# Four early first-layer tiles between the id transposes and the block's end, twelve spread over the gate steps

## The chip, the cores and the metric

The kernel runs on one core of a Trainium2 chip. The time is the device time of one execution in microseconds; lower is better. The engines are TensorE (PE, its weight loads PEld), VectorE (DVE), ScalarE (ACT), GpSimd (POOL) and SyncE (SP); the last three issue transfers.

## What is computed

One decoder layer on 256 prompt rows and 64 sample rows: projections, two kinds of attention, an output projection with LayerNorm, and then PEER, a retrieval over 128 x 128 single-neuron experts. The change lies in PEER:

```python
q = (xc @ wq).reshape(PEER_CHUNK, PEER_HEADS, PEER_DK)
s1, s2 = q[..., :half] @ k1, q[..., half:] @ k2        # scores, top 16 of each, top 16 of their sums
experts = jnp.take_along_axis(cidx, sel, axis=-1)       # 8 heads x 16 expert ids a row
g = jax.nn.softmax(sc, axis=-1)
hid = jax.nn.gelu(jnp.einsum('ced,cd->ce', u_tab[experts], xc))
y = jnp.einsum('ce,ced->cd', g * hid, v_tab[experts])
```

## The kernel before, in words

For the prompt rows the kernel does not gather experts. It multiplies x with all of u (the first layer, 128 tiles of 128 experts, each a weight tile of 128 x 1024 values), applies gelu, multiplies with a gate matrix W that is zero where a row did not choose an expert, and multiplies with all of v. The program is a series of blocks. In each block every engine has its own instruction stream, held together by semaphores, and a block's end is at the source line of the class that follows, L1096 in the profile.

`route_block` finds ids and gates. TensorE makes the queries (L1203) and scores (L1212); VectorE and GpSimd pick the best (L1313 to L1351) and VectorE adds up ids (`expert_ids`, L1328). TensorE then turns ids and gates (L1225, L1226) into PSUM, from where VectorE copies them (L1371 to L1374) and splits them into integers in the small instructions L1387 to L1396, which are the last of the block on VectorE.

TensorE has time to spare in this block, so it computes part of the first layer early, in plain float32: `early_hidden` (L1079) makes one tile in eight matmuls (sixteen records in the trace), `early_out` on ScalarE copies it out of PSUM (L1088) and stores it in DRAM (L1090). There are EARLY = 32 such tiles. The first EARLY_R = 16 are in `route_block`, all ahead of the turned ids; their weights are loaded by SP into four slots of `big` (L1142), tile n once tile n-4 is done.

`expert_block` begins with the gate phase: 32 steps, in four groups of eight, that build W from one-hot matrices. In step c VectorE makes the one-hots (L1694 once, L1698 eight times), TensorE multiplies them (`gate_rows`, L1557), ScalarE copies the result into W (L1628). One-hots have two buffers and PSUM has two slots. The semaphore `c_mm` starts at 2 and counts gate steps done by TensorE; these lines tie the engines:

```python
ve.wait_ge(s["c_mm"], c + 1)      # onehots(c): gate step c-2 is done
pe.wait_ge(s["onehot"], c + 1)    # gate_rows(c): its one-hots are there
pe.wait_ge(s["W_out"], c + 1)     # gate_rows(c): step c-2 is copied out
act.wait_ge(s[f"st_w{g - 2}"], 64)  # group g writes W where group g-2 lay, once that is stored
```

The other 16 early tiles are done here, one behind every second gate step (behind steps 1, 3, 5 and 7 of a group). Their weights come through GpSimd's queue (`early_u`, L1789), behind four gathers. Behind group 0 and group 1, SP stores that group's half of W to DRAM (L1487). Behind group 1 TensorE also does one ordinary first-layer tile (L1584 to L1586). After the last step come another ordinary tile (L1532 to L1534) and five matmuls that zero the accumulators (L1592). Then the product phase begins, in which each of 128 steps needs its early or ordinary hidden tile, its rows of W and a tile of v (L1544). Its first hidden tiles are early ones, which SP reads back (L1477) once all 32 early tiles are stored; VectorE multiplies them with W (L1727, L1728) when the zeroing matmuls (`y_mm`) and all copies into W are done.

Of the kernel before, what the change touches and what calls it, by code (L numbers as in the profile page):

```python
# [29 lines left out]
P = 128  # L30
# [975 lines left out]
HH = 2 * NH  # L1006
# [61 lines left out]
        eng.tensor_tensor(y, y, self.lnp[0:r, 1, c], ALU.add).then_inc(s[end], 1)  # L1068


EARLY, EARLY_R = 32, 16


def early_hidden(pe, t, s, n, m, u):
# [18 lines left out]
def route_block(nc, d, t, s):  # L1093


    with ExitStack() as ctx:  # L1096
# [24 lines left out]
        bv = sb("best_vals", [P, HU, TOPK])  # L1121
        ids = sb("expert_ids", [P, HU, TOPK])
# [7 lines left out]
        block = ctx.enter_context(nc.Block())  # L1130
        OT, x1, ident = t.OT, t.x1, t.c0[:, 0:P]
        bank = lambda i: t.psum[:, i]
        norm = Norm(s, 0, lambda i: xr[0:RT[i], i, :], lambda i, h: bank(2 * i + h)[0:RT[i], :], lambda i: x1[0:RT[i], i, :], ln, bn, mv)


# [3 lines left out]
        after_unit = {4: 0, 5: 1, 6: 2}  # L1139
# [31 lines left out]
        @block.tensor  # L1171
        def _(pe):
            def early(n):
                pe.wait_ge(s[f"ld_p{n % 4}"], 16 * (n // 4 + 1))
                early_hidden(pe, t, s, n, n % 2, t.big[:, n % 4 * D:(n % 4 + 1) * D])

            for i in range(TILES):
                r = slice(P * i, P * i + RT[i])
                for h in range(2):
                    for k in range(KD):  # L1180
                        if i == 0 and h == 0 and k % 4 == 0:
                            pe.wait_ge(s[f"ld_wo{k // 4}"], 32)
                        mm = pe.matmul(bank(2 * i + h)[0:RT[i], :], OT[:, k, r], wo[:, k, 512 * h:512 * (h + 1)],
                                       start=(k == 0), stop=(k == KD - 1))
                mm.then_inc(s["o_mm"], 1)
            for x in range(2 * TILES):
                i = x // 2
                pe.wait_ge(s["ln_r" if x % 2 else "ln_l"], i + 1)
                if x >= 2:
                    pe.wait_ge(s["x_out"], x - 1)  # L1190
                for y in range(4):
                    k = 4 * (x % 2) + y
                    mm = pe.transpose(bank(6 + x % 2)[:, y * P:y * P + RT[i]], x1[0:RT[i], i, k * P:(k + 1) * P], ident[0:RT[i], 0:RT[i]])
                mm.then_inc(s["x_turn"], 1)
            pe.wait_ge(s["x_out"], 6)
            pe.wait_ge(s["ld_ky"], 32)
            for g in range(4):
                for j in range(4 * g, 4 * g + 4):
                    pe.wait_ge(s[f"ld_wq{j % 4}"], 16 * (j // 4 + 1))
                    if j >= 2:  # L1200
                        pe.wait_ge(s["q_out"], j - 1)
                    for k in range(KD):
                        mm = pe.matmul(bank(j % 2)[:, 0:ROWS], wq[:, j % 4, k, :], xT[:, k, :], start=(k == 0), stop=(k == KD - 1))  # L1203
                    mm.then_inc(s["q_mm"], 1)
                pe.wait_ge(s["q_out"], 4 * g + 4)
                for i, l in by_group[g]:
                    u = units.index((i, l))
                    if u >= 2:
                        pe.wait_ge(s["sc_out"], u - 1)
                    for j in range(4):  # L1210
                        for r0, q in ([(0, 4 * l + j)] if i < 2 else [(0, 4 * l + j), (64, 4 * l + 8 + j)]):
                            mm = pe.matmul(bank(2 + u % 2)[r0:r0 + RT[i], j * P:(j + 1) * P], qT[:, q, P * i:P * i + RT[i]], ky[:, q, :],  # L1212
                                           start=True, stop=True)
                    mm.then_inc(s["sc_mm"], 1)
                    if u in after_unit:
                        early(after_unit[u])
            for n in range(len(after_unit), EARLY_R):
                early(n)
            pe.wait_ge(s["hp_out"], EARLY_R)
            pe.wait_ge(s["id_sum"], len(units))  # L1220
            pe.wait_ge(s["g_fin"], 1)
            for i in range(TILES):
                h = slice(8 * i, min(8 * i + 8, HU))
                n = 16 * (h.stop - h.start)
                pe.transpose(bank(4 + i)[0:n, 0:P], ids[:, h].rearrange("p h k -> p (h k)"), ident)  # L1225
                pe.transpose(bank(4 + i)[0:n, P:2 * P], bv[:, h].rearrange("p h k -> p (h k)"), ident).then_inc(s["id_turn"], 1)  # L1226

        @block.scalar
        def _(act):
# [9 lines left out]
            for g in range(4):  # L1239
# [10 lines left out]
                        early_out(act, d, t, s, after_unit[u], after_unit[u] % 2)  # L1250
                if g == 0:
                    act.activation(t.x1h[:], xT[:, :, 0:SEQ], ACT.Copy).then_inc(s["x_hi"], 1)
            for n in range(len(after_unit), EARLY_R):
                early_out(act, d, t, s, n, n % 2)
            act.wait_ge(s["g_sub"], 1)
            act.activation(bv[:], bv[:], ACT.Exp).then_inc(s["g_exp"], 1)

        @block.gpsimd
        def _(gp):
# [38 lines left out]
        def _(ve):  # L1298
# [31 lines left out]
            for u in range(len(units)):  # L1330
                q = u % 2
# [33 lines left out]
            for i in range(TILES):  # L1365
                r = slice(P * i, P * i + RT[i])
                ve.wait_ge(s["id_turn"], i + 1)
                for x, dst in enumerate((cT, gT)):
                    o = bank(4 + i)[:, x * P:(x + 1) * P]
                    if i < 2:  # L1370
                        ins = ve.tensor_copy(dst[:, r], o)  # L1371
                    else:
                        ve.tensor_copy(dst[0:64, r], o[0:64, 0:64])
                        ins = ve.tensor_copy(dst[64:P, r], o[0:64, 64:P])  # L1374
                ins.then_inc(s["id_out"], 1)
# [35 lines left out]
def expert_block(nc, d, t, s):  # L1411
# [6 lines left out]
    with ExitStack() as ctx:  # L1418
# [33 lines left out]
        norm = Norm(s, TILES, x1, sums, x1, ln, bn, mv)  # L1452
        x1h, x1l = t.x1h, t.x1l
        GROUPS, STEPS = SEQ // GRP, GRP // GT
        NU = NE - EARLY
        POS = NE // UP

# [65 lines left out]
        def _(pe):  # L1523
# [47 lines left out]
                mm.then_inc(s["v_mm"], 1)  # L1571

            for g in range(GROUPS):
                with pe.Fori(0, STEPS // 4) as i:
                    for x in range(2):
                        for q in range(2):
                            gate_rows(i * 4 + (STEPS * g + 2 * x + q), q)
                        pe.wait_ge(s[f"ld_e{x}"], i * 16 + (32 * g + 16))
                        early_hidden(pe, t, s, i * 2 + (EARLY_R + 4 * g + x), x, up[:, x])
                if g == 1:  # L1580
                    pe.wait_ge(s["u_lo"], 1)
                    for k in range(KD):
# [31 lines left out]
        def _(act):  # L1614
# [24 lines left out]
            for g in range(GROUPS):  # L1639
                if g >= 2:  # L1640
                    act.wait_ge(s[f"st_w{g - 2}"], 64)
                with act.Fori(0, STEPS // 4) as i:
                    for x in range(2):
                        for q in range(2):
                            W_out(i * 4 + (STEPS * g + 2 * x + q), g, i * (4 * GT) + (2 * x + q) * GT, q)
                        early_out(act, d, t, s, i * 2 + (EARLY_R + 4 * g + x), x, i * 16 + (8 * EARLY_R + 32 * g))
                if g == 0:
                    u_hi(0, 16)
                    u_hi(1, 16)
                if g == 1:  # L1650
                    hidden(0, 0)
# [334 lines left out]
```

## Time and profile before

| | us |
|---|---|
| three timed runs | 1536.66, 1536.66, 1539.16 |
| median | 1536.66 |
| the profiled execution | 1539.63 |
| its span | 1537.80 |
| its mean granted TensorE clock | 0.945 of full |

The span is what the trace covers; 1.83 us lie around it. Times in rows of the trace are counted from the start of the span. A row of the timeline names the line of the source, the engine, and in brackets how long the engine stood idle and what released it. In a row by windows, PEclk 1.00 is the clock of 2.4 GHz and 0.50 is 1.2 GHz. The profiled execution took 2.97 us more than the median of the three runs.

### The profile page before, as it was taken

Reading aid. Unit: us, or ns where it says so; the run is one execution under the profiler, and the core shown is the slowest. Engines: PE = TensorE matmul, PEld = TensorE weight load, DVE = VectorE, ACT = ScalarE, POOL = GpSimd, SP = SyncE. Lnnn points to the kernel's source line nnn. Section 1 sums busy time; section 2 is a strip of 40 time slices with the busy share of each in tenths; the row PEclk is TensorE's granted clock in tenths of the full one; section 3 lists DMA queues with packets and bytes.
Section 4 is the critical chain, followed back from the end, with each engine's and each line's share of the span. In section 5 each row is a group of like instructions: output and inputs, shape, how many; then the busy total and the mean of one; then the engine's idle time right before and its main releaser. Section 6 shows DMA issues by size and latency. Waiting matters only on the chain.

```text
span 1537.8 us, 26735 instructions
## 1 busy us (share of the span) xinstructions
PE 1403.0 (91%) x8955; PEld 1150.1 (75%) x8956; DVE 871.2 (57%) x2128; ACT 527.7 (34%) x1002; POOL 288.1 (19%) x557
## 2 busy tenths in 40 slices
PE   7979997878888989994999999999999999999974
PEld 6869897554456456783998888999987888888853
DVE  3440001765443319975996788888885555555436
ACT  3411001543332111111333454544454444444422
POOL 0112222200000116651000111111111122211222
PEclk9989998788888989997999999999999999999987
DMA  7877887403887314353792999999996888888861
GB/s 241 296 243 251 303 285 263 172 1 127 304 318 270 144 53 155 101 164 147 187 245 80 309 315 314 314 313 319 314 314 212 286 289 294 281 275 286 296 210 64
DMA packets 158045, 359.55 MB, mean 234 GB/s; under 512 B 50579, under 2 KB 92435, under 8 KB 154259
## 3 DMA queue, kind: packets, MB, share of 16 engines
q1 hardware_dynamic: 125970, 239.37, 46.5%
q0 software_dynamic: 25088, 112.93, 21.0%
q10 hardware_dynamic: 6912, 6.29, 1.2%
q8 instruction: 42, 0.69, 0.2%
q14 instruction: 33, 0.26, 0.1%
HBM read 342.08 MB, written 53.61 MB: 257 GB/s over the span
## 4 chain that ended last, share of the span: by engine, by line
PE 50%; DVE 1%; DMA 1%; POOL 1%; issue 0%; ACT 0%; DVEq 0%; ACTq 0%; SPq 0%; POOLq 0%
PE psum L1544 23%; PE psum L1534 6%; PE psum L1533 6%; PE psum L1532 6%; PE psum L1079 4%; PE psum L1557 3%; PE psum L1569 2%; DMA early_u<-in_peer_u 1%; DMA gathered<-in_peer_v,v_rows_of 0%; POOL gathered L1775 0%; DVE ln_bn L1034 0%; DVE x L1068 0%; DVE x L1029 0%; POOL gathered L1780 0%; DVE x L1066 0%
## 5 line engine op out<-in xcount | busy, mean ns | idle before, releaser
L1707 DVE TENSOR_TENSOR v_lo<-big,v_hi 128x1024 fp32r<-128x1024 f32 x128 | 156.8, 1225 | 115.5 <-ACT v_hi L1624 91.6
L1533 PE MATMUL psum<-x_lo,u_hi 128*128 128x256 f32 x760 | 215.0, 283 | 0.0
L1534 PE MATMUL psum<-x_hi,u_lo 128*128 128x256 f32 x760 | 215.0, 283 | 0.0
L1532 PE MATMUL psum<-x_hi,u_hi 128*128 128x256 f32 x760 | 214.8, 283 | 0.0
L1624 ACT ACTIVATE v_hi<-big 128x1024 fp32r<-128x1024 f32 x128 | 135.3, 1057 | 140.2 <-PE psum L1544 108.9
L1544 PE MATMUL psum<-v_hi,gated_hi 128*128 128x512 f32 x512 | 162.6, 399 | 6.7 <-DVE gated_lo L1732 6.7
L1544 PE MATMUL psum<-v_lo,gated_hi 128*128 128x512 f32 x512 | 160.1, 394 | 0.0
L1544 PE MATMUL psum<-v_hi,gated_lo 128*128 128x512 f32 x512 | 159.4, 393 | 0.0
L1533 PEld LDWEIGHTS psum<-x_lo,u_hi 128*128 128x128 f32 x760 | 145.5, 191 | 3.7
L1532 PEld LDWEIGHTS psum<-x_hi,u_hi 128*128 128x128 f32 x760 | 145.5, 191 | 3.7
L1534 PEld LDWEIGHTS psum<-x_hi,u_lo 128*128 128x128 f32 x760 | 145.5, 191 | 0.0
L1703 DVE TENSOR_TENSOR u_lo<-big,u_hi 128x1024 fp32r<-128x1024 f32 x96 | 117.0, 1219 | 0.0
L1544 PEld LDWEIGHTS psum<-v_hi,gated_hi 128*128 128x128 f32 x512 | 90.8, 191 | 34.3 <-issue 13.1
L1775 POOL DMA_INDIRECT gathered<-in_peer_u_rows,u_rows_of x64 | 61.8, 966 | 278.8 <-DVE sample_h L1739 256.3
L1544 PEld LDWEIGHTS psum<-v_lo,gated_hi 128*128 128x128 f32 x512 | 97.2, 190 | 21.5
L1544 PEld LDWEIGHTS psum<-v_hi,gated_lo 128*128 128x128 f32 x512 | 97.2, 190 | 21.2
L1780 POOL DMA_INDIRECT gathered<-in_peer_v,v_rows_of x64 | 61.1, 955 | 274.2 <-PE psum L1569 242.8
L1619 ACT ACTIVATE u_hi<-big 128x1024 fp32r<-128x1024 f32 x96 | 100.4, 1047 | 0.8 <-ACT early_hidden L1088 0.8
L1633 ACT ACTIVATE big<-psum 128x256 f32<-128x256 f32 x96 | 36.5, 380 | 159.4 <-PE psum L1534 157.4
L1739 DVE CUSTOM_DVE_ANT_0 products<-gathered,x 128x1024 bf16<-128x1024 f32 x64 | 78.0, 1219 | 0.0
L1203 PE MATMUL psum<-x1T,wq_ring 128*128 128x320 f32 x256 | 72.1, 444 | 0.5 <-ACT x1T L1236 0.5
L394 PE MATMUL psum<-cmp_pages,w1k 128*128 128x128 f32 (+1 forms) x512 | 64.0, 287 | 8.4 <-DMA cmp_pages<-in_cmp_pool 5.0
(308 smaller groups left out, 2401.6 us busy)
## 6 DMA issues: line engine op xcount, KB each, us to landing
big<-in_peer_v SPq DMA_DIRECT2D x128, 512.0 KB
big<-in_peer_u SPq DMA_DIRECT2D x112, 512.0 KB, 3.9
big<-in_a_k SPq DMA_DIRECT2D x8, 2048.0 KB, 11.9
a_vals<-in_a_v SPq DMA_DIRECT2D x8, 2048.0 KB
keep_ak<-in_a_k POOLq DMA_DIRECT2D x32, 508.0 KB, 6.2
keep_av<-in_a_v POOLq DMA_DIRECT2D x24, 512.0 KB, 6.7
sel_pages<-in_sel_pool SPq DMA_DIRECT2D x64, 128.0 KB, 2.8
wq_ring<-in_peer_wq SPq DMA_DIRECT2D x16, 512.0 KB, 3.7
```

The costliest lines, as they stand in the source:

```text
L394: mm = pe.matmul(o.rearrange("p k (g b) -> p k g b", b=8), w1[a][:, c, h * P:(h + 1) * P], rhs, start=(c == 0), stop=(c == CMP_W1 - 1), sk ...
L1203: mm = pe.matmul(bank(j % 2)[:, 0:ROWS], wq[:, j % 4, k, :], xT[:, k, :], start=(k == 0), stop=(k == KD - 1))
L1532: pe.matmul(H[:, 0:SEQ], uh[:, q, kc], x1h[:, k, :], start=(k == 0), stop=False)
L1533: pe.matmul(H[:, 0:SEQ], uh[:, q, kc], x1l[:, k, :], start=False, stop=False)
L1534: mm = pe.matmul(H[:, 0:SEQ], ul[:, q, kc], x1h[:, k, :], start=False, stop=(k == KD - 1))
L1544: mm = pe.matmul(bank(2 * i + h), a[:, q, r], b[:, q, 512 * h:512 * (h + 1)], start=False, stop=stop and x == 2, skip_group_check=True)
L1619: act.activation(uh[:, q], us[:, q], ACT.Copy).then_inc(s["u_hi"], 1)
L1624: act.activation(vh[:, q], vs[:, q], ACT.Copy).then_inc(s["v_hi"], 1)
L1703: ve.tensor_tensor(ul[:, q], us[:, q], uh[:, q].bitcast(F32), ALU.subtract).then_inc(s["u_lo"], 1)
L1707: ve.tensor_tensor(vl[:, q], vs[:, q], vh[:, q].bitcast(F32), ALU.subtract).then_inc(s["v_lo"], 1)
L1739: ve.tensor_tensor_reduce(junk[:], gr[:, k % 4], t.x1[:, 2, :], 1.0, 0.0, ALU.mult, ALU.add, h4[:, k % 4:k % 4 + 1]).then_inc(s["dots"], 1)
L1775: gp.indirect_dma_start(gr[:, m % UN, :], None, d.peer_u_rows, bass.IndirectOffsetOnAxis(t.uix[:, m:m + 1], 0))\
```

## The change

Twenty tiles instead of sixteen are in `route_block`. Sixteen of them stay where they are; four stand behind the transposes that turn the ids. The transposes write into banks 0, 1 and 4 instead of 4, 5 and 6, since the early tiles use banks 5 and 7, and no longer wait until the early tiles are copied out. In the gate phase the twelve other tiles stand behind steps 1, 4 and 6 of each group, and its loops on TensorE and ScalarE are written out.

```diff
-EARLY, EARLY_R = 32, 16
+EARLY, EARLY_R, EARLY_T = 32, 20, 4
...
+        turned = [bank(0), bank(1), bank(4)]
...
-            for n in range(len(after_unit), EARLY_R):
+            for n in range(len(after_unit), EARLY_R - EARLY_T):
                 early(n)
-            pe.wait_ge(s["hp_out"], EARLY_R)
+            pe.wait_ge(s["q_out"], HH)
+            pe.wait_ge(s["x_out"], 6)
             pe.wait_ge(s["id_sum"], len(units))
             pe.wait_ge(s["g_fin"], 1)
...
+            for n in range(EARLY_R - EARLY_T, EARLY_R):
+                early(n)
...
             act.activation(bv[:], bv[:], ACT.Exp).then_inc(s["g_exp"], 1)
+            for n in range(EARLY_R - EARLY_T, EARLY_R):
+                early_out(act, d, t, s, n, n % 2)
...
+        EARLY_AT = [1, 4, 6]
...
-                with pe.Fori(0, STEPS // 4) as i:
-                    for x in range(2):
-                        for q in range(2):
-                            gate_rows(i * 4 + (STEPS * g + 2 * x + q), q)
-                        pe.wait_ge(s[f"ld_e{x}"], i * 16 + (32 * g + 16))
-                        early_hidden(pe, t, s, i * 2 + (EARLY_R + 4 * g + x), x, up[:, x])
+                for c in range(STEPS):
+                    gate_rows(STEPS * g + c, c % 2)
+                    if c in EARLY_AT:
+                        n = EARLY_R + len(EARLY_AT) * g + EARLY_AT.index(c)
+                        pe.wait_ge(s[f"ld_e{n % 2}"], 16 * ((n - EARLY_R) // 2 + 1))
+                        early_hidden(pe, t, s, n, n % 2, up[:, n % 2])
```

ScalarE's loop over the gate steps is changed in the same way, with `early_out` behind steps 1, 4 and 6.

TensorE around the turned ids and the first gate steps, before (L1225 and L1226 turn ids and gates, L1096 is the block's end, L1557 with x8 is one gate step, L1079 an early tile):

```order
L1225 MATMUL psum<-c,expert_ids 64x128
L1226 MATMUL psum<-c,best_vals 64x128
L1096 UNCONDITIONAL_BRANCH
L1522 UNCONDITIONAL_BRANCH
L1574 UNCONDITIONAL_BRANCH
L1574 ISA
L1557 MATMUL psum<-OT,gated_i 128x128 x8
L1554 REGISTER_ALU
L1557 MATMUL psum<-OT,gated_i 128x128 x8
L1578 ISA
L1077 ISA
L1079 MATMUL psum<-x1T,early_u 128x256 x8
```

The same place and the first group's later steps in the changed kernel, whose lines are numbered two to eight higher (L1227, L1228 and L1565 are the transposes and the gate steps):

```order
L1227 MATMUL psum<-c,expert_ids 64x128
L1228 MATMUL psum<-c,best_vals 64x128
L1079 MATMUL psum<-x1T,big 128x256 x32
L1096 UNCONDITIONAL_BRANCH
L1530 UNCONDITIONAL_BRANCH
L1565 MATMUL psum<-OT,gated_i 128x128 x16
L1079 MATMUL psum<-x1T,early_u 128x256 x8
L1565 MATMUL psum<-OT,gated_i 128x128 x24
L1079 MATMUL psum<-x1T,early_u 128x256 x8
L1565 MATMUL psum<-OT,gated_i 128x128 x16
L1079 MATMUL psum<-x1T,early_u 128x256 x8
```

The four tiles (x32) stand between the last transpose and the block's end, and the gate phase has runs of two, three, two and three steps between tiles where it had runs of two.

ScalarE at the end of the block, before (L1256 is the exponential of the gates, L1613 the start of the next block):

```order
L1256 ACT_TABLE_LOAD
L1256 ACTIVATE best_vals<-best_vals 128x320
L1096 UNCONDITIONAL_BRANCH
L1613 UNCONDITIONAL_BRANCH
```

And in the changed kernel, where the exponential is L1260 and the next block starts at L1621:

```order
L1260 ACT_TABLE_LOAD
L1260 ACTIVATE best_vals<-best_vals 128x320
L1088 ACTIVATE early_hidden<-psum 128x256
L1090 DMA early_hidden_of<-early_hidden 128x256
...
L1088 ACTIVATE early_hidden<-psum 128x256
L1090 DMA early_hidden_of<-early_hidden 128x256
L1096 UNCONDITIONAL_BRANCH
L1621 UNCONDITIONAL_BRANCH
```

Four copies and four stores, of which the first and the last pair are shown, stand between the exponential and the block's end.

## Rows read from the trace of the kernel before

**Rows 1.** Windows by stage; the first row names the columns.
```profile
core 0: us, PE busy (x) PEld busy (x) DVE busy (x) ACT busy (x) POOL busy (x), PEclk, DMA share, GB/s
705.50:843.40 137.90, 123.58 (x820) 115.27 (x821) 108.12 (x296) 45.00 (x56) 14.13 (x21) 0.95 0.62 179
843.40:1537.80 694.40, 660.16 (x4049) 569.58 (x4049) 453.46 (x764) 309.98 (x497) 135.96 (x192) 0.97 0.82 278
```

**Rows 2.** Timeline, route block's end: start, length, engine, line, what, idle and releaser.
```profile
690.39 0.38 ACT L1088 ACTIVATE early_hidden<-psum 128x256 f32<-128x256 f32 x1 [3.07 <-PE psum L1079]
693.85 0.38 ACT L1088 ACTIVATE early_hidden<-psum 128x256 f32<-128x256 f32 x1 [3.07 <-PE psum L1079]
...
699.58 0.45 PE L1225 MATMUL psum<-c,expert_ids 128*128 128x128 f32 x1 [5.77 <-DVE expert_ids L1328]
...
700.67 0.42 PE L1226 MATMUL psum<-c,best_vals 128*64 128x128 f32 x1
...
704.73 0.29 DVE L1396 COPY gates_of<-gates_turned 128x256 f32<-128x256 f32 x1
```

**Rows 3.** Records at the block's end (L1096): nanoseconds, then first and last start.
```profile
L1096 PEldq DRAIN  x1: 1543/1543/1543, 699.6 to 699.6; - x1
...
L1096 ACTq EVENT_SEMAPHORE  x1: 17/17/17, 705.5 to 705.5; - x1
...
L1096 PEldq EVENT_SEMAPHORE  x1: 51/51/51, 705.5 to 705.5; - x1
```

**Rows 4.** Timeline, start of the expert block to its first early tile.
```profile
709.69 5.29 PE L1557 MATMUL psum<-OT,gated_i 128*128 128x128 f32 x32 [8.59 <-DVE gated_i L1698]
...
721.51 5.73 PEld L1079 LDWEIGHTS psum<-x1T,early_u 128*128 128x128 f32 x16 [6.72 <-issue]
...
727.26 3.76 PEld L1557 LDWEIGHTS psum<-OT,gated_i 128*128 128x128 f32 x32
...
727.77 0.38 ACT L1088 ACTIVATE early_hidden<-psum 128x256 f32<-128x256 f32 x1 [11.63 <-PE psum L1079]
...
728.33 0.36 ACTq L1090 DMA_DIRECT2D early_hidden_of<-early_hidden  x1
729.58 1.23 DVE L1694 TENSOR_TENSOR OT<-big,i 128x1024 f32<-128x1024 f32 x1 [9.78 <-PE psum L1557]
```

**Rows 5.** Timeline, one period of the gate phase.
```profile
734.29 3.76 PEld L1557 LDWEIGHTS psum<-OT,gated_i 128*128 128x128 f32 x32
...
736.61 1.23 DVE L1694 TENSOR_TENSOR OT<-big,i 128x1024 f32<-128x1024 f32 x1 [0.56 <-PE psum L1557]
...
737.97 3.33 PEld L1079 LDWEIGHTS psum<-x1T,early_u 128*128 128x128 f32 x16
...
739.80 1.22 DVE L1694 TENSOR_TENSOR OT<-big,i 128x1024 f32<-128x1024 f32 x1
740.93 2.14 DVE L1698 TENSOR_SCALAR gated_i<-big,i,gates_of 128x128 f32<-128x128 f32 x8
```

**Rows 6.** Timeline, the end of the gate phase.
```profile
835.53 0.19 PEld L1532 LDWEIGHTS psum<-x_hi,u_hi 128*128 128x128 f32 x1
...
838.85 1.03 PE L1592 MATMUL psum<-products 128*128 128x512 bf16 x4
840.97 0.29 DVE L1727 TENSOR_TENSOR big<-early_hidden,gate_tile 128x128 f32<-128x128 f32 x1 [10.72 <-ACT early_hidden L1637]
...
843.41 1.22 PE L1544 MATMUL psum<-v_hi,gated_hi 128*128 128x512 f32 x2 [3.54 <-DVE gated_lo L1732]
```

**Rows 7.** Timeline, stores of W's second half, and SP's first work behind them.
```profile
774.55 16.47 SPq L1487 DMA_DIRECT2D gate_w<-gate_matrix  x4
...
800.00 0.83 SPq L1474 DMA_DIRECT2D gate_tile<-gate_w  x2
```

**Rows 8.** Windows around pauses of TensorE, for its granted clock.
```profile
185.50:188.00 2.50, 0.00 (x0) 0.00 (x0) 0.11 (x1) 0.10 (x1) 1.80 (x4) 1.00 0.77 284
188.00:195.00 7.00, 6.92 (x62) 6.92 (x63) 0.00 (x0) 0.00 (x0) 0.00 (x0) 1.00 0.87 284
378.50:380.20 1.70, 0.00 (x0) 0.00 (x0) 1.60 (x6) 1.70 (x4) 0.00 (x0) 1.00 0.47 131
382.00:385.00 3.00, 3.00 (x6) 1.01 (x6) 0.68 (x1) 1.36 (x9) 0.00 (x0) 0.50 0.99 415
...
843.40:849.00 5.60, 5.59 (x13) 4.44 (x14) 5.60 (x11) 1.65 (x4) 1.11 (x2) 0.50 0.80 240
```

More of the change, by code:

```diff
@@ L1224, in _ @@
                 n = 16 * (h.stop - h.start)
-                pe.transpose(bank(4 + i)[0:n, 0:P], ids[:, h].rearrange("p h k -> p (h k)"), ident)
-                pe.transpose(bank(4 + i)[0:n, P:2 * P], bv[:, h].rearrange("p h k -> p (h k)"), ident).then_inc(s["id_turn"], 1)
+                pe.transpose(turned[i][0:n, 0:P], ids[:, h].rearrange("p h k -> p (h k)"), ident)
+                pe.transpose(turned[i][0:n, P:2 * P], bv[:, h].rearrange("p h k -> p (h k)"), ident).then_inc(s["id_turn"], 1)
+            for n in range(EARLY_R - EARLY_T, EARLY_R):
+                early(n)
         @block.scalar
@@ L1252, in _ @@
                     act.activation(t.x1h[:], xT[:, :, 0:SEQ], ACT.Copy).then_inc(s["x_hi"], 1)
-            for n in range(len(after_unit), EARLY_R):
+            for n in range(len(after_unit), EARLY_R - EARLY_T):
                 early_out(act, d, t, s, n, n % 2)
@@ L1368, in _ @@
                 for x, dst in enumerate((cT, gT)):
-                    o = bank(4 + i)[:, x * P:(x + 1) * P]
+                    o = turned[i][:, x * P:(x + 1) * P]
                     if i < 2:
@@ L1454, in expert_block @@
         GROUPS, STEPS = SEQ // GRP, GRP // GT
+        EARLY_AT = [1, 4, 6]
+        assert EARLY == EARLY_R + GROUPS * len(EARLY_AT)
         NU = NE - EARLY
@@ L1641, in _ @@
                     act.wait_ge(s[f"st_w{g - 2}"], 64)
[L1642 to L1646, printed above, removed]
+                for c in range(STEPS):
+                    W_out(STEPS * g + c, g, c * GT, c % 2)
+                    if c in EARLY_AT:
+                        n = EARLY_R + len(EARLY_AT) * g + EARLY_AT.index(c)
+                        early_out(act, d, t, s, n, n % 2)
                 if g == 0:
```

## The prediction

> **What bounds the kernel now.** I read the windows by stage first: after the route block come 137.90 us of gate phase and then 694.40 us of product phase, in which TensorE works nearly all the time [rows 1]. Both edits lie ahead of the product phase and leave all 32 early tiles done, so what counts is when the first product starts: 843.41 in this trace [rows 6]. Whatever moves that moment moves the end.
>
> Then the timeline at the route block's end. TensorE idles 5.77 us, turns ids and gates from 699.58, has its last transpose from 700.67 to 701.09, and idles 8.59 us up to the first gate step at 709.69 [rows 2, 4]. In that gap VectorE works to 705.02 (704.73 + 0.29) [rows 2]. The records of the block's end say what follows: the semaphore event of ScalarE and TensorE comes at 705.5, though TensorE had drained by 701.1 [rows 3]. The idle engines wait for the slowest one, which today is VectorE: the end of the block is a barrier over all of them.
>
> Then one period of the gate phase. Two gate steps on TensorE take 3.68 us (734.29 to 737.97), so 1.84 each; the tile takes the rest of a period of 7.03, 3.35 us (727.26 to 734.29 is one period) [rows 4, 5]. VectorE starts new one-hots 0.48 us after the gate step that frees the buffer (734.29 + 1.84 = 736.13, start 736.61), makes a set every 3.19 us (736.61 to 739.80), and a set is ready to use 3.27 us after its start (740.93 + 2.14 = 743.07 less 739.80); with 0.05 us to TensorE I take 3.32 [rows 5]. TensorE never waits and VectorE idles 0.56 us a period.
>
> **Part 1, four tiles behind the transposes.** They begin at 700.9, as the last transpose clears. Their weights are there: the slots are free once tiles 12 to 15 are done, the last by about 693.8 [rows 2], 7 us earlier. In the route block a tile takes 3.46 us (690.39 to 693.85) [rows 2]. The clock is low there: the first tile after an idle stretch in the gate phase took 5.75 us (721.51 to 727.26) [rows 4], and I take that for the first of these. So TensorE is done at 700.9 + 5.75 + 3 x 3.46 = 717.0. ScalarE then copies and issues the store: from 727.26, where TensorE had gone on, to 728.33 + 0.36 = 728.69 it took 1.43 us [rows 4]. The block's last engine is done at 718.45 instead of 705.02: **+13.4 us**. Everything behind the barrier moves with it, the four gathers and GpSimd's load of the first tile too, so the wait for that load, to 721.51 in the trace [rows 4], only moves. Bounds of this term: all four tiles at full clock give 13.8 instead of 16.1 us and a term of +11.1; a clock low for 5.6 us as at 843.40 [rows 8] costs 2.8 instead of 2.3, so +13.9.
>
> **Part 2, the spread over the gate phase.** I count from T, the end of a tile that stands behind step c. Gate step c+1 ends at T + 1.84. Only then may VectorE begin the one-hots of c+3: start T + 2.32, ready T + 5.64. Step c+2 has long been ready and ends at T + 3.68. With a tile behind every second step this never showed; with three steps in a run, TensorE waits from T + 3.68 to T + 5.64, 1.96 us, then does step c+3 (to 7.48) and the tile (to 10.83). A run of two still takes 7.03. A group has now two runs of three and one of two, 28.7 us, against 4 x 7.03 = 28.1 before: three tiles instead of four, and no time won. The fourth tile's 3.35 us goes into two waits.
>
> From the end of the first tile (727.26) to that of the last, before, was 108.3 us (835.53 less 727.26 [rows 4, 6]). Now: four groups with 10.83 + 7.03, and between groups 10.83 twice and once 12.6, where the ordinary tile behind step 15 takes 2.96 us more (108.3 less 15 x 7.03, within 0.1) and covers the wait in part: 71.4 + 34.3 = 105.7. So −2.6 us. Behind the last tile stood 7.88 us to the first product [rows 6]. Now step 31 stands behind it too. The zeroing matmuls end at 838.85 + 1.03 = 839.88, 4.35 us after the tile; now 1.84 later, 6.19, and VectorE, which waits for them, starts 0.1 us on at 6.3 instead of 5.44 (840.97) [rows 6]. With 2.44 us from there to the product it is 8.7. **Part 2 is −2.6 + 0.85 = −1.7 us.**
>
> **What I cost at nothing, and its cover.** The other banks and waits of the transposes (long fulfilled). The written-out loops. The store of W: SP's next step came 25.4 us after the store began (774.55 to 800.00) [rows 7]; now the group that writes over it is copied some 32 us (first half) and 31 us (second) after the store begins, so 6 us of cover remain; what a store is late beyond that is lost whole. ScalarE's two conversions of u at group 0's end lie beside the first steps of group 1, one of which waits for one-hots anyway.
>
> **The clock.** TensorE now pauses 1.96 us eight times. After a pause of at least 1.70 us at 378.50 the clock was 0.50 in 382.00 to 385.00, 3.0 us at half speed, so 1.5 us lost; after one of 2.50 us at 185.50 it stayed 1.00 [rows 8]. Price from 0 to 8 x 1.5 = 12 us. The steps around these pauses are dense as at 188, so I stay near the low end and take one fall, +1.5. At the end the pause ahead of the first product shrinks from 3.54 to 2.5 us, and the 5.6 us at 0.50 that follow it [rows 8] may stay away, up to −2.8; I do not count it. In "TensorE: Matmul & The Clock Gate", in its table of practical rules, the Trainium skill advises no idle gaps above about 3 us between bursts. By that rule the eight pauses cost nothing and the last one keeps the clock: the sum would be 4.3 us less. The pause at 378.50 does not agree with it, the one at 185.50 does.
>
> **Sum.** 13.4 − 1.7 + 1.5 = +13.2 us. On the profiled execution that is 1539.63 + 13.2 = 1552.8. The median of the runs shown is 2.97 lower, so I predict 1536.66 + 13.2 = 1549.9.
>
> **Rivals.**
>
> *The gate phase runs at the pace of its busiest engine.* Without the two waits, VectorE's 3.19 us a step would set it. Its set for step 4 starts at 729.58, 2.3 us behind the first tile's end [rows 4]; 28 sets and the 2.4 us for u_lo end 91.7 later, gate step 31 by 96.0, the zeroing by 100.4, the product at 102.9, where mine comes at 105.7 + 8.7 = 114.4. That is 11.5 us less and gives 1536.66 + 13.4 − 1.7 − 11.5 = 1536.9, no change. For it speaks that VectorE has 108.12 us of work in 137.90 [rows 1]; against it, that each set must wait for a TensorE step. [...] Chance 0.07.
>
> *The barrier does not hold the next block back (the other side).* Then TensorE goes from the tiles at 717.0 into the first two gate steps, whose one-hots are ready, and is done at 720.7, ahead of the load at 721.51. Part 1 costs nothing, and the clock, having worked from 700.9, is high at the first gate-phase tile: 3.46 instead of 5.75, −2.3. With part 2, −4.0, and with −2.8 at the first product down to −6.8, so 1529.9 to 1532.7. It decides as soon as the tiles' end costs the other engines less than about 1 us instead of 13.4. Against it stand the events at 705.5 [rows 3]. Chance 0.04.
>
> *The clock falls at most pauses.* 8 x 1.5 instead of 1.5: 1536.66 + 11.7 + 12 = 1560.4. Chance 0.06.
>
> *The store of W is late.* Past its 6 us of cover, say by 4 us in each of the two groups: 1557.9. Chance 0.02.
>
> **Chances and range.** My forecast has 0.81. Its own bounds: low, part 1 at +11.1, no fall, and −2.8 at the end: +6.6, 1543.3; high, part 1 at 13.9 and four falls: +18.2, 1554.9. I draw the range from 1543.3 to 1557.5, which also takes in most of the late store and some of the clock rival, and leaves out about 0.15. A change of 0.2%, 3.1 us, is about what a measurement of this kernel can tell from none. Slower: 0.81 + 0.06 + 0.02 = 0.89. Same: 0.07. Faster: 0.04.
>
> **What the changed profile would show.** Right: the events of the block's end at about 719, with ScalarE's store as the last work ahead; VectorE idle from 705 to 719; TensorE pauses of about 2 us released by L1698's successor in each run of three steps, periods 10.8 and 7.0; the last early tile about 106 us after the first; the first product near 855. Wrong: first one-hots soon after 706 (no barrier); steps 3.2 us apart without pauses (the pace rival); PEclk near 0.8 in the gate phase (clock rival); ScalarE idle at step 16 or 24 until a transfer lands (store rival).

## The result: 7 us slower, half of what was forecast

| | us |
|---|---|
| before, median of 20 runs | 1536.83 (1532.51 to 1544.47) |
| after, median of 20 runs | 1543.43 (1539.02 to 1551.95) |
| ratio after to before, with its 95% interval | 1.0046 [1.0031, 1.0061] |
| profiled execution of after, its span | 1543.7 |

The ratio is +7.1 us (+4.8 to +9.4). The change is slower, as forecast; the forecast of 1549.9 was 6.5 us too high, and its range, from 1543.3, holds the median by 0.1 us.

The stretches ahead of the route block's first early tile differ by some us from one execution to the next, in code that nobody touched. So I count from that tile (615.2 in the trace before, 614.7 after), and I compare the block's end at L1096 and the first product of the last phase:

| kernel | block's end after first tile | block's end to first product | both |
|---|---|---|---|
| before | 90.3 | 137.9 | 228.2 |
| after | 101.6 | 134.4 | 236.0 |

The block's end came 11.3 us later, the gate phase gave 3.5 back, and the product phase starts 7.8 us later.

The timeline of after, the end of the route block (start, length, engine, line, what, idle time and its releaser), against [rows 2]:

```profile
695.84 0.49 DVE L1365 TENSOR_REDUCE gate_sum<-best_vals 128x20 f32<-128x320 f32 x1 [14.83 <-ACT best_vals L1260]
...
699.15 0.45 PE L1227 MATMUL psum<-c,expert_ids 128*128 128x128 f32 x1 [5.93 <-DVE expert_ids L1334]
...
700.46 14.72 PE L1079 MATMUL psum<-x1T,big 128*128 128x256 f32 x64
...
704.30 0.29 DVE L1402 COPY gates_of<-gates_turned 128x256 f32<-128x256 f32 x1
...
715.22 0.38 ACT L1088 ACTIVATE early_hidden<-psum 128x256 f32<-128x256 f32 x1 [3.07 <-PE psum L1079]
...
715.63 0.34 ACTq L1090 DMA_DIRECT2D early_hidden_of<-early_hidden  x1
...
716.54 0.27 DVE L1694 MEMSET products<- 128x256 uint32 x1 [11.94 <-PEq L1096]
```

The four moved tiles are one run of 14.72 us, to 715.18. ScalarE's copy and store follow, to 715.97, and VectorE, done at 704.6, stands idle for 11.94 us. Four records of the block's end in after, against [rows 3]:

```profile
L1096 DVEq DRAIN  x1: 19/19/19, 704.8 to 704.8; - x1
...
L1096 ACTq DRAIN  x1: 158/158/158, 716.0 to 716.0; - x1
...
L1096 ACTq EVENT_SEMAPHORE  x1: 17/17/17, 716.3 to 716.3; - x1
...
L1096 PEldq EVENT_SEMAPHORE  x1: 51/51/51, 716.3 to 716.3; - x1
```

VectorE has drained at 704.8 and is let go at 716.3 with the others: the last engine is now ScalarE instead of VectorE.

TensorE's timeline in the gate phase of after (L1565 is a gate step, 16 records each; L1079 a tile), against [rows 4, 5]:

```profile
720.55 6.35 PE L1565 MATMUL psum<-OT,gated_i 128*128 128x128 f32 x32 [5.37 <-DVE gated_i L1706]
730.99 6.23 PE L1079 MATMUL psum<-x1T,early_u 128*128 128x256 f32 x16 [4.08 <-DMA early_u<-in_peer_u]
...
742.49 2.05 PE L1565 MATMUL psum<-OT,gated_i 128*128 128x128 f32 x16 [1.70 <-DVE gated_i L1706]
744.38 3.62 PE L1079 MATMUL psum<-x1T,early_u 128*128 128x256 f32 x16
747.83 3.73 PE L1565 MATMUL psum<-OT,gated_i 128*128 128x128 f32 x32
751.40 3.62 PE L1079 MATMUL psum<-x1T,early_u 128*128 128x256 f32 x16
754.86 3.73 PE L1565 MATMUL psum<-OT,gated_i 128*128 128x128 f32 x32
760.29 2.05 PE L1565 MATMUL psum<-OT,gated_i 128*128 128x128 f32 x16 [1.70 <-DVE gated_i L1706]
```

A run of two steps and its tile take 7.03 us (747.83 to 754.86). The run of three takes 10.8 (737.05 to 747.83) and has a pause of 1.70 for the one-hots ahead of its third step. There are seven such pauses, six of 1.70 and, behind the ordinary tile, one of 0.44. The pauses and the end of the phase, in the chief waits and then the timeline of after (waits: engine and line, releaser, us in total, times, longest), against [rows 6]:

```profile
PE psum L1565 <- DVE gated_i L1706: 16.0, 8, 5.4
```

```profile
842.21 1.95 PE L1565 MATMUL psum<-OT,gated_i 128*128 128x128 f32 x16
846.87 1.25 PE L1600 MATMUL psum<-products 128*128 128x512 bf16 x5
848.63 0.29 DVE L1735 TENSOR_TENSOR big<-early_hidden,gate_tile 128x128 f32<-128x128 f32 x1 [8.06 <-PE psum L1600]
850.73 0.72 PE L1552 MATMUL psum<-v_hi,gated_hi 128*128 128x512 f32 x2 [2.60 <-DVE gated_lo L1740]
```

The gate step behind the last early tile begins at 842.21, 105.2 us after the one behind the first (737.05). By the weight loads, which the prediction counted from, it is 842.00 less 736.84, the same 105.2, and the product follows 8.7 us later.

Windows of after for the granted clock (PEclk is the third figure from the right), against [rows 8]:

```profile
core 0: us, PE busy (x) PEld busy (x) DVE busy (x) ACT busy (x) POOL busy (x), PEclk, DMA share, GB/s
...
740.00:748.00 8.00, 6.30 (x42) 5.70 (x41) 8.00 (x25) 2.11 (x3) 0.00 (x0) 1.00 0.09 36
...
756.00:764.00 8.00, 6.30 (x49) 5.90 (x48) 7.44 (x21) 4.85 (x5) 0.00 (x0) 1.00 0.80 220
850.70:856.30 5.60, 5.57 (x17) 4.43 (x18) 5.60 (x12) 2.69 (x4) 1.09 (x2) 0.70 0.83 251
...
699.00:700.40 1.40, 1.25 (x6) 1.21 (x7) 0.55 (x3) 0.00 (x0) 0.00 (x0) 0.50 0.04 12
700.40:703.00 2.60, 2.60 (x11) 2.20 (x10) 2.39 (x11) 0.00 (x0) 0.00 (x0) 0.70 0.00 0
703.00:706.00 3.00, 3.00 (x16) 2.64 (x15) 1.42 (x6) 0.38 (x1) 0.00 (x0) 1.00 0.00 0
```

The first two hold pauses and show the full clock, as do all other windows between 738 and 850. The first moved tile has 0.70 on the mean for 2.6 us only, and the first product 0.70 where it had 0.50.

### The profile page after: what moved, and what is told of

Read it like the earlier page. It is cut to its first block, busy times and chain, and to the rows that moved or that the text cites. A ratio compares the mean times of both kernels' runs of the same rounds, so it can differ in the third digit from the quotient of the medians.

```text
span 1543.7 us, 26545 instructions
## 1 busy us (share of the span) xinstructions
PE 1403.6 (91%) x8956; PEld 1150.5 (75%) x8956; DVE 871.0 (56%) x2128; ACT 527.8 (34%) x1002; POOL 285.9 (19%) x553
## 4 chain that ended last, share of the span: by engine, by line
PE 48%; DVE 2%; issue 1%; DMA 1%; POOL 1%; DVEq 0%; ACT 0%; POOLq 0%
PE psum L1552 23%; PE psum L1542 6%; PE psum L1541 6%; PE psum L1540 6%; PE psum L1079 3%; PE psum L1565 3%; PE psum L1577 2%; DVE gated_i L1706 1%; DMA early_u<-in_peer_u 0%; DMA gathered<-in_peer_v,v_rows_of 0%; DVEq L1706 0%; POOL gathered L1783 0%; DVE ln_bn L1034 0%; DVE x L1068 0%; DVE x L1029 0%
## 5 line engine op out<-in xcount | busy, mean ns | idle before, releaser
L1552 PEld LDWEIGHTS psum<-v_hi,gated_hi 128*128 128x128 f32 x512 | 90.5, 190 | 33.6 <-issue 13.4
L1565 PE MATMUL psum<-OT,gated_i 128*128 128x128 f32 x512 | 63.9, 283 | 16.0 <-DVE gated_i L1706 16.0
L1565 PEld LDWEIGHTS psum<-OT,gated_i 128*128 128x128 f32 x512 | 62.3, 199 | 18.4 <-DVE gated_i L1706 17.7
```

Of the source, the lines that this page charges most:

```text
L1552: mm = pe.matmul(bank(2 * i + h), a[:, q, r], b[:, q, 512 * h:512 * (h + 1)], start=False, stop=stop and x == 2, skip_group_check=True)
L1565: mm = pe.matmul(out[:, r * NE:(r + 1) * NE], A[:, q, r, :], E[:, q, r, :], start=True, stop=True)
```

## The experiments

Each was timed in five rounds beside the kernel before (twelve runs each, but seven of e6_both and six of f2_all). In the rows of expert-block edits, `early_part(n)` emits the next n of the early tiles' matmuls (eight make a tile), so that a list says how many stand behind each gate step.

The table collects what the profiles show, counted as above, and the timed ratios. The profile columns come from one execution each: e1_tiles_behind has the gate phase of before, and takes 135.7 us for it instead of 137.9 (its first load lands 1.3 us sooner behind the block's end, and its first tile takes 4.9 us instead of 5.75). So a difference of some 2 us in the gate phase cannot be read as the effect of an edit by itself. The block's ends repeat better: 90.3 to 90.4 in the three kernels with the route block of before, 101.6 to 101.9 in the three with that of after. The early tiles are given as ahead of the transposes / behind them / in the expert block.

| kernel | tiles | block's end | to product | both | ratio to before |
|---|---|---|---|---|---|
| before | 16 / 0 / 16 | 90.3 | 137.9 | 228.2 | |
| after | 16 / 4 / 12 | 101.6 | 134.4 | 236.0 | 1.0046 [1.0031, 1.0061] |
| e1_tiles_behind | 12 / 4 / 16 | 90.3 | 135.7 | 226.0 | 0.9989 [0.9967, 1.0011] |
| e2_spread_alone | 16 / 0 / 12 | 92.5 | 134.5 | 227.0 | 0.9993 [0.9974, 1.0012] |
| e3_thirds | 16 / 4 / 12 | 101.8 | 124.2 | 226.0 | 0.9969 [0.9947, 0.9992] |
| e4_tiles_after_barrier | 16 / 0 / 16 | 90.4 | 136.9 | 227.3 | 0.9994 [0.9976, 1.0013] |
| e5_pattern_135 | 16 / 4 / 12 | 101.9 | 130.9 | 232.8 | 1.0006 [0.9982, 1.0031] |
| f1_exp_earlier | 14 / 2 / 16 | 80.6 | 137.5 | 218.1 | 0.9941 [0.9917, 0.9964] |
| f3_after_exp_earlier | 16 / 4 / 12 | 94.2 | 133.2 | 227.4 | 1.0012 [0.9987, 1.0037] |
| e6_both | 16 / 0 / 16 | 90.3 | 124.6 | 214.9 | 0.9931 [0.9898, 0.9964] |
| f2_all | 14 / 2 / 16 | 80.5 | 123.1 | 203.6 | 0.9865 [0.9835, 0.9894] |

**e1_tiles_behind.** **Four of the sixteen tiles behind the transposes, nothing else** (from before, with the banks and waits of the change):

```diff
-EARLY, EARLY_R = 32, 16
+EARLY, EARLY_R, EARLY_T = 32, 16, 4
...
-            for n in range(len(after_unit), EARLY_R):
+            for n in range(len(after_unit), EARLY_R - EARLY_T):
                 early(n)
...
+            for n in range(EARLY_R - EARLY_T, EARLY_R):
+                early(n)
...
             act.activation(bv[:], bv[:], ACT.Exp).then_inc(s["g_exp"], 1)
+            for n in range(EARLY_R - EARLY_T, EARLY_R):
+                early_out(act, d, t, s, n, n % 2)
```

> The first part alone: of the sixteen tiles of the route block the last four stand behind the turned ids; the gate phase keeps its sixteen tiles behind every second step. Theory (the block's end waits for them): 10 to 11.5 us slower than before, block's end at about 716 instead of 705.5, first product 10 to 11.5 us later. Rival (the block's end costs little and the loss comes from the gate phase): 0 to 2 us slower.

Measured: no change, 0.9989, and the block's end at 90.3 as before. The expectation fell. Its timeline says why:

```profile
681.06 0.47 ACT L1260 ACTIVATE best_vals<-best_vals 128x320 f32<-128x320 f32 x1
681.56 0.49 DVE L1365 TENSOR_REDUCE gate_sum<-best_vals 128x20 f32<-128x320 f32 x1 [0.97 <-ACT best_vals L1260]
...
685.84 0.45 PE L1227 MATMUL psum<-c,expert_ids 128*128 128x128 f32 x1 [6.90 <-DVE expert_ids L1334]
...
704.74 0.27 DVE L1692 MEMSET products<- 128x256 uint32 x1 [13.45 <-PEq L1096]
```

The exponential stands in ScalarE's queue behind the copies of all tiles that are ahead of the transposes. In after (the first row of its timeline above) sixteen stand there and VectorE waits 14.83 us; so it does in the kernel before:

```profile
696.42 0.49 DVE L1359 TENSOR_REDUCE gate_sum<-best_vals 128x20 f32<-128x320 f32 x1 [14.83 <-ACT best_vals L1256]
```

With twelve it waits 0.97. The transposes then come at 71.6 us after the first tile instead of 84.4, and the four tiles, 16.2 us, fill the 12.7 us won and the time in which VectorE worked behind the transposes; that this comes out at the same 90.3 is chance. VectorE is still held 13.45 us at the block's end. So there is a barrier, but four tiles behind the transposes cost nothing when four fewer stand ahead; what costs in after is their number in this block, 20 instead of 16. That opened a question: does the exponential's place cost the kernel before time?

**e2_spread_alone.** **The spread alone.** The changed kernel without the work of its four tiles behind the transposes: the store sends what the buffer holds, so those four tiles are stale, and SP does not load their weights. The four stores stand ahead of the exponential here, not behind it.

```diff
-            for n in range(EARLY_R - EARLY_T, EARLY_R):
-                early(n)
+            pe.wait_ge(s["hp_out"], EARLY_R - EARLY_T)
+            pe.sem_inc(s["hp_mm"], EARLY_T)
...
+            for n in range(EARLY_R - EARLY_T, EARLY_R):
+                act.dma_start(d.early[n], t.hp[:, n % 2]).then_inc(s[f"st_h{n % 2}"], 16)
+            act.sem_inc(s["hp_out"], EARLY_T)
             act.wait_ge(s["g_sub"], 1)
             act.activation(bv[:], bv[:], ACT.Exp).then_inc(s["g_exp"], 1)
-            for n in range(EARLY_R - EARLY_T, EARLY_R):
-                early_out(act, d, t, s, n, n % 2)
```

> The second part alone: twelve tiles behind steps 1, 4 and 6; the four tiles behind the turned ids are left out (not computed; stale values are stored for them), so that the block's end is as before. Theory (each run of three steps makes TensorE wait 2 us): 1 to 3 us faster than before, periods of 10.8 and 7.0 us. Rival (the gate phase follows its busiest engine once four tiles are gone): 10 to 13 us faster, steps 3.2 us apart.

Measured: 227.0, 1.2 us less than before, ratio 0.9993. The block's end is not as before, as was expected, but 2.2 us later. The four stores hold up the exponential, and VectorE waits 16.86 us for it instead of 14.83:

```profile
696.03 1.94 ACTq L1260 DMA_DIRECT2D early_hidden_of<-early_hidden  x4
...
699.88 0.49 DVE L1366 TENSOR_REDUCE gate_sum<-best_vals 128x20 f32<-128x320 f32 x1 [16.86 <-ACT best_vals L1263]
```

So the spread is read from the gate phase alone. It takes 134.5, as in after: with four tiles fewer than before, 13.4 us of TensorE work at 3.35, it is 3.4 us shorter, where the pace rival needs 10 to 13. Its chief wait is the one that the prediction put there:

```profile
PE psum L1566 <- DVE gated_i L1707: 19.3, 8, 8.6
```

**e3_thirds.** **Single matmuls instead of whole tiles in the gate phase** (from after):

```diff
-        EARLY_AT = [1, 4, 6]
+        QUOTA = [0, 0, 8, 3, 3, 3, 3, 3, 3, 3, 3, 3, 3, 3, 3, 3,
+                 3, 3, 3, 3, 3, 3, 3, 3, 3, 3, 3, 3, 3, 3, 3, 4, 0]
...
-                    if c in EARLY_AT:
-                        n = EARLY_R + len(EARLY_AT) * g + EARLY_AT.index(c)
-                        pe.wait_ge(s[f"ld_e{n % 2}"], 16 * ((n - EARLY_R) // 2 + 1))
-                        early_hidden(pe, t, s, n, n % 2, up[:, n % 2])
+                    early_part(QUOTA[STEPS * g + c + 1])
```

> The changed kernel with its twelve gate-phase tiles cut into single matmuls: the first tile whole behind step 1, then three matmuls (four behind the second) behind each step up to step 30. Theory (TensorE waits because a whole tile delays the step that frees the one-hot buffer): no pause above 0.5 us in the steps, VectorE sets 3.2 us apart, 10 to 12 us faster than the changed kernel, so 3 to 5 us faster than before. Rival (the waits have another cause, a copy into W or the conversion of u): no faster than the changed kernel by more than 3 us.

Measured: 124.2 us instead of 134.4 from the block's end to the product, and the whole kernel is 0.9969 of before. TensorE's only wait for one-hots left is the first:

```profile
PE psum L1568 <- DVE gated_i L1728: 5.4, 1, 5.4
```

Its steps come evenly, at VectorE's pace of 3.19 us:

```profile
760.36 2.05 PE L1568 MATMUL psum<-OT,gated_i 128*128 128x128 f32 x16
762.25 1.46 PE L1600 MATMUL psum<-x1T,early_u 128*128 128x256 f32 x6
763.55 2.05 PE L1568 MATMUL psum<-OT,gated_i 128*128 128x128 f32 x16
765.44 1.46 PE L1600 MATMUL psum<-x1T,early_u 128*128 128x256 f32 x6
766.74 2.05 PE L1568 MATMUL psum<-OT,gated_i 128*128 128x128 f32 x16
```

So the pace rival's time is to be had with the same twelve tiles, but not while whole tiles stand between steps. A whole tile ahead of a step frees that step's buffer 3.35 us later, and VectorE is late by that.

**e5_pattern_135.** **Other places, behind steps 1, 3 and 5 of each group** (from after, the same code with this list):

```diff
+        QUOTA = [0, 0, 8, 0, 8, 0, 8, 0, 0, 0, 8, 0, 8, 0, 8, 0, 0,
+                 0, 8, 0, 8, 0, 8, 0, 0, 0, 8, 0, 8, 0, 8, 0, 0]
```

> The changed kernel with its twelve tiles behind steps 1, 3 and 5 of each group instead of 1, 4 and 6: runs of two, two and four steps. From the period rule (a run of two 7.03 us, of three 10.8, and of four 10.8 + 3.19 = 14.0): 28.1 us a group instead of 28.6 and a shorter last stretch, 2 to 4 us faster than the changed kernel, 3 to 5 us slower than before. Rival (only the number of tiles counts): no difference from the changed kernel.

Measured: 3.2 us less than after to the product and 4.6 more than before; the ratio is 1.0006. Its timeline, of weight loads, shows a run of four steps (759.67 to 773.64, 13.97 us) beside a run of two (752.64 to 759.67):

```profile
752.64 3.76 PEld L1568 LDWEIGHTS psum<-OT,gated_i 128*128 128x128 f32 x32
756.32 3.33 PEld L1600 LDWEIGHTS psum<-x1T,early_u 128*128 128x128 f32 x16
759.67 3.76 PEld L1568 LDWEIGHTS psum<-OT,gated_i 128*128 128x128 f32 x32
765.32 1.86 PEld L1568 LDWEIGHTS psum<-OT,gated_i 128*128 128x128 f32 x16 [1.89 <-DVE gated_i L1728]
768.51 1.86 PEld L1568 LDWEIGHTS psum<-OT,gated_i 128*128 128x128 f32 x16 [1.33 <-DVE gated_i L1728]
...
773.64 3.76 PEld L1568 LDWEIGHTS psum<-OT,gated_i 128*128 128x128 f32 x32
```

One run of four and two of two in a group (28.0) cost less than the changed kernel's two of three and one of two (28.6). The model of one buffer freed by one step gives both, and with them the whole of the 3.5 us by which this gate phase is shorter (130.9 against 134.4). From the end of the first tile to that of the last stand three runs of four and eight of two, 99.7 us, against seven of three and four of two, 105.2. Behind the last tile stand two gate steps instead of one, 10.5 us to the product against 8.7. The time, 0.9 us above before with an interval from −2.8 to +4.8, agrees with the profile's 4.6 but doesn't prove it.

**e4_tiles_after_barrier.** **The four tiles behind the block's end** (from after: none behind the transposes, four at the head of the gate phase):

```diff
-EARLY, EARLY_R, EARLY_T = 32, 20, 4
+EARLY, EARLY_R, EARLY_T, EARLY_X = 32, 20, 0, 4
...
+            early_part(QUOTA[0])
```

with `QUOTA[0] = 32`, and with SP's loads into the four slots held back until the tiles in them are done.

> The changed kernel with the four tiles one block later: TensorE does them first in the expert block, while VectorE makes the first one-hots, and SP's four loads into the slots that they read wait for them. Theory (only the block's end made them dear): about 9 us faster than the changed kernel, 1 to 4 us faster than before. Rival (they delay the first gate steps, or the held-back loads come late, as much as they delayed the block's end): within 3 us of the changed kernel.

Measured: the block's end is back at 90.4, and the product comes 8.7 us sooner than in after, at no change from before (0.9994; by the ratios it is 8 us faster than after). Behind the block's end the same four tiles cost 2.5 us (136.9 against 134.4):

```profile
702.37 15.80 PE L1603 MATMUL psum<-x1T,big 128*128 128x256 f32 x64 [4.93 <-PEq L1096]
```

They lie where TensorE in after waited 5.37 us for the first one-hots and 4.08 for the first load, and the tile behind the second gate step takes 3.5 us here (721.57 to 725.03) instead of 5.8. Ahead of the block's end the four cost 11.3. Against the kernel before nothing is won: the spread tiles still stand whole, and what that costs the runs with cut tiles show.

**f1_exp_earlier.** **The exponential earlier** (from before: on ScalarE behind the copy of the twelfth tile, and the transposes on TensorE two tiles earlier):

```diff
-EARLY, EARLY_R = 32, 16
+EARLY, EARLY_R, EARLY_T = 32, 16, 2
...
-            for n in range(len(after_unit), EARLY_R):
+            for n in range(len(after_unit), 12):
                 early_out(act, d, t, s, n, n % 2)
             act.wait_ge(s["g_sub"], 1)
             act.activation(bv[:], bv[:], ACT.Exp).then_inc(s["g_exp"], 1)
+            for n in range(12, EARLY_R - EARLY_T):
+                early_out(act, d, t, s, n, n % 2)
```

> The kernel before with its gate phase untouched, sixteen tiles in the route block, but ScalarE's exponential ahead of the copy of tile 12 instead of behind that of tile 15, and the turned ids between tiles 13 and 14. New theory (the exponential waits in ScalarE's queue behind the tiles' copies and holds VectorE, then TensorE and the block's end): TensorE does the sixteen tiles without the 5.8 us pause, the block ends at about 697 instead of 705.5 counted from the same start, 8 to 9 us faster than before. Rival (VectorE's and GpSimd's own chain ends late anyway): less than 3 us faster.

Measured: 0.9941, 9.1 us faster than before, with the block's end 9.7 us sooner. This run moves two things, the exponential and, by two tiles, the transposes. The next one moves the exponential alone. VectorE's wait of 14.83 is 0.95, TensorE's of 5.77 ahead of the transposes is gone, and tiles follow them at once:

```profile
677.26 0.49 DVE L1367 TENSOR_REDUCE gate_sum<-best_vals 128x20 f32<-128x320 f32 x1 [0.95 <-ACT best_vals L1260]
...
681.58 0.30 PE L1227 MATMUL psum<-c,expert_ids 128*128 128x128 f32 x1
...
682.26 7.07 PE L1079 MATMUL psum<-x1T,big 128*128 128x256 f32 x32
```

**f3_after_exp_earlier.** **The same on the changed kernel:**

```diff
-            for n in range(len(after_unit), EARLY_R - EARLY_T):
+            for n in range(len(after_unit), 12):
                 early_out(act, d, t, s, n, n % 2)
             act.wait_ge(s["g_sub"], 1)
             act.activation(bv[:], bv[:], ACT.Exp).then_inc(s["g_exp"], 1)
+            for n in range(12, EARLY_R - EARLY_T):
+                early_out(act, d, t, s, n, n % 2)
```

> The changed kernel with the same move of the exponential and nothing else: sixteen tiles ahead of the turned ids, four behind. New theory: ids and gates are ready when tile 15 ends, the transposes follow at once, and the block ends 5 to 6 us earlier than in the changed kernel, so 5 to 6 us faster than it and 1 to 3 us slower than before. Rival (the four tiles cost what they cost through something else than the block's end): no change against the changed kernel.

Measured: the block's end 7.4 us sooner than in after, the product 8.6, and the whole within the noise of before (1.0012, by the ratios 5 us faster than after). So the question left by the first experiment is answered: in the changed kernel the exponential's place alone held the block's end back by 7.4 us. In the kernel before it was moved only together with the transposes, for 9.7. With the idle time around the turned ids gone, 20 tiles still cost more than 16 in this block (94.2 against 80.6), 13.6, about the plain work of four tiles (4 x 3.46 = 13.8).

**e6_both.** **Nothing behind the transposes, four tiles at the head of the gate phase, the rest cut into single matmuls** (from after):

```diff
-EARLY, EARLY_R, EARLY_T = 32, 20, 4
+EARLY, EARLY_R, EARLY_T, EARLY_X = 32, 20, 0, 4
...
+        QUOTA = [8, 8, 8, 3, 4, 3, 4, 3, 4, 4, 3, 4, 3, 4, 4, 3, 4,
+                 3, 4, 3, 4, 4, 3, 4, 3, 4, 4, 3, 4, 3, 4, 4, 0]
```

> Route block as before with sixteen tiles; sixteen tiles in the expert block: four read the slots of the route block (one ahead of gate step 0, one behind each of the steps 0 and 1, and on), all others cut into single matmuls, three or four behind each step. Theory (TensorE then never pauses from the block's start to the product phase): 11 to 14 us faster than before. Rival (the pauses at the start of the gate phase belong to gathers and loads that come late whatever TensorE does): under 6 us faster.

Measured: 0.9931, 10.6 us faster, a little under the 11 to 14 expected, and 13.3 to the product. TensorE does pause once ahead of the last gate step, 4.93 us at the block's end. The gate phase with all sixteen tiles takes 124.6 instead of 137.9.

**f2_all.** **Both at once: this gate phase and the earlier exponential** (from the kernel of the last experiment):

```diff
-EARLY, EARLY_R, EARLY_T, EARLY_X = 32, 20, 0, 4
+EARLY, EARLY_R, EARLY_T, EARLY_X = 32, 20, 2, 4
...
-            for n in range(len(after_unit), EARLY_R - EARLY_T - EARLY_X):
+            for n in range(len(after_unit), 12):
...
+            for n in range(12, EARLY_R - EARLY_T - EARLY_X):
+                early_out(act, d, t, s, n, n % 2)
```

> Both together: exponential earlier, turned ids between tiles 13 and 14, four tiles behind the block's end, single matmuls between the gate steps. If the two gains add up: 19 to 23 us faster than before. If one covers the other (a load or a store of W becomes the bound): not more than the better of the two, 11 to 14 us.

Measured: 1514.43 us, 0.9865 of before, 20.7 us faster. The two gains add: 10.1 and 13.3 to the product make 23.4, measured 24.6; by the timed runs 9.1 and 10.6 make 19.7, measured 20.7. A window of this kernel, from its block's end to its first product:

```profile
694.90:818.00 123.10, 119.92 (x821) 111.88 (x821) 108.12 (x296) 44.42 (x56) 12.04 (x17) 1.00 0.65 189
```

TensorE does the same work as in [rows 1] (821 weight loads in both) and is busy in 119.92 of 123.10 us; it is the bound of this phase, with a mean clock of 1.00.

## Why the prediction was right, and what was mis-sized

**Direction and mechanism: right.** The event records moved with ScalarE's last store, VectorE idled from 704.6 to 716.5, and undoing this one thing (the four tiles behind the block's end) gave 8.7 us back. That the end is a barrier is shown by the changed kernel's profile and by the experiment of four tiles behind the transposes alone. The size is not a hit: 7.1 us against 13.2. Five terms erred, all to the same side: part 1 by 2.1 us, the clock by 1.5, the start of the products by 1.4, the load that I said only moves by 1.3, part 2 by 0.6. The median lies at the lower bound, +6.6, which I had worked out from part 1 at full clock, no fall of the clock and 2.8 us back at the first products. That it still falls inside the range is in part luck.

**Part 1, +13.4 forecast, +11.3 measured: the mis-sized term.** The transposes came 84.4 us after the first tile in both kernels, as assumed. The four tiles took 14.7 us instead of 16.1: I gave the first of them 5.75, the length of a tile after a long pause in the gate phase, but it took 4.3 (14.72 less 3 x 3.46), and the clock was back at 1.00 by 702. The copy and store ended 0.8 us behind the last matmul (715.18 to 715.97) instead of the 1.43, which I had counted from the next weight load. In the experiment with twelve tiles ahead, TensorE had been idle 6.90 us instead of 5.93, and the four took 16.2 us (687.15 to ScalarE's copy of the last at 703.43), so the assumed price does occur. Why the clock rose sooner here I cannot say. The step also missed something that did not enter its sum: what costs is that the block has twenty tiles instead of sixteen, not that four stand behind the transposes.

**Part 2, −1.7 forecast.** The mechanism is shown: periods of 10.8 and 7.03, a wait at each run of three steps, no pace of 3.19 until the tiles are cut up. Between first and last tile 105.2 us were measured for 105.7, behind the last tile 8.7 for 8.7; together −2.3. In pricing the clock I counted eight pauses; there are seven, as the sum over the runs had them. TensorE's matmuls pause 1.70 us, its weight loads 1.89, for the 1.96 that I counted between weight loads.

**What I said only moves: 1.3 us off.** The first load landed 14.7 us behind the block's end (730.99 less 716.3), where it was 16.0. GpSimd issued it equally late (723.63 and, before, 712.77, so 7.3 us each), and from issue to use it was 7.4 instead of 8.7 us. In the other kernels that wait for this load it landed 14.6 (f3_after_exp_earlier) to 15.9 us (e3_thirds) behind the block's end, so 1.3 us may be no effect of the change. What makes the transfer faster or slower wasn't tried.

**The clock, +1.5 forecast, nothing measured.** Through six pauses of 1.70 us the windows of the gate phase show 1.00. Here the traces agree with the Trainium skill's "TensorE: Matmul & The Clock Gate", table under "Why this matters for your kernels", against idle gaps above about 3 us. Ahead of the first product they do not: that pause was 2.60 us, and the clock, still 1.00 from 850.7 to 852.0, was 0.50 from 853.0 to 855.0. Over the 5.6 us from 850.7 the mean is 0.70, where it had been 0.50: of the 2.8 us that I left uncounted, 1.1 came back.

Sum to the first product: 11.3 − 1.3 − 3.1 + 0.9 = 7.8, as the trace has it; from there to the span's end 693.0 us instead of 694.4. That makes 6.4, and the timed difference is 7.1 (4.8 to 9.4).

**The rivals.** *The pace of the busiest engine*: refuted for this change (seven pauses; with the four tiles left out the gate phase was 3.4 us shorter than before, not the 13.2 of this rival), and its time was reached once the tiles were cut. *No barrier*: refuted by the event records. *The clock falls at most pauses*: refuted. *A late store of W*: SP's read of W, which waits for both stores, came at 809.2, 22.7 us behind the start of the second (before, at 800.00, 25.4; an issue of a tile of u stands between in both), and no wait of ScalarE for it stands among the chief waits.

## What to carry to other kernels

Filler work that stands whole between steps with two buffers delays the step that frees the next buffer by its full length: cut it to the size of the slack of one step (3 to 4 of a tile's 8 matmuls here, 10 us) before asking how many pieces there are. Before a block's end, what every engine waits for is the longest chain, so work that one engine "has time for" belongs behind the barrier, in the next block's starting waits, if it is last here. And look in each engine's own queue for an instruction that others wait for behind copies that nobody waits for: in the kernel before, moving one exponential, and the transposes two tiles up with it, was worth 9 us, more than the change under study cost.

## What the hardware showed that was not expected

Pauses of nearly equal length did not have one effect. After at least 1.70 us at 378.50 the clock was 0.50 from 382.0 to 385.0 [rows 8], but it had still been 1.00 from 380.2 to 381.0, so that this pause made it fall is not shown; after six pauses of 1.70 between dense gate steps it was 1.00. After pauses of 5.93 and 6.90 us ahead of the transposes it was 0.50, and it was back at 1.00 by 702.0, 2.9 us after work resumed, in the first case; in the second it was still 0.50 from 690 to 691, 5.2 us on, and back by 692:

```profile
687.00:690.00 3.00, 3.00 (x9) 2.47 (x8) 2.75 (x13) 0.00 (x0) 0.00 (x0) 0.50 0.00 0
690.00:695.00 5.00, 5.00 (x20) 4.25 (x20) 1.15 (x5) 0.38 (x1) 0.00 (x0) 0.83 0.08 26
695.00:703.00 8.00, 8.00 (x38) 7.03 (x37) 0.00 (x0) 0.77 (x2) 0.00 (x0) 1.00 0.10 35
```

These are windows of the kernel with twelve tiles ahead of the transposes. The end of a low stretch was as variable as its start.
